# Reordering a head's products in a recurrence and moving a small decay computation two products later in a Fourier stage

## The chip, the cores and the metric

The kernel runs on one core of one Trainium2 chip, in one launch. The metric is the device time in microseconds (us), taken as the median of repeated executions. TensorE is called PE in the rows, VectorE DVE, ScalarE ACT, GpSimd POOL; SyncE (SP) issues the weight loads.

## The reference

Two transformer blocks in float32 on 512 tokens with 16 meta tokens ahead (length L = 528, width 1024). The first block has a forgetting attention (8 heads of 64), a gated linear recurrence (8 heads of 128), and a mixture of 32 experts. The second has a feed-forward layer, a hybrid mixer (a Fourier branch, a short convolution, a two-way gated delta net), and a second feed-forward layer. Two parts matter here.

```python
# the recurrence of the first block, per head of 128; chunks of 64 tokens
f_val = lb + (1.0 - lb) * sigmoid(f_h);  log_f = log(f_val);  k = 1.0 - f_val
q = q_h * 128 ** -0.5;  v = i_h
b = cumsum(log_f, axis=1)                      # within a chunk
o_inter = einsum('bchk,bhkv->bchv', q * exp(b), state)
scores  = sum(q[:, :, None] * k[:, None] * decay, -1)
new_state = exp(b_last)[..., None] * state + einsum('bshk,bshv->bhkv', k_dec, v)
o = rms_norm(o, hgrn_norm_w) * sigmoid(g_h)
# the decays of the second block's delta net, from two small projections
beta = sigmoid(beta_logit);  g = -exp(A_log) * softplus(alpha_logit + dt_bias);  gc = cumsum(g)
```

## The kernel before, in words

**Engines and queues.** Each engine has its own list of instructions, written by a function of its own (`..._pe`, `..._act`, `..._dve`), and runs it in order; semaphores join them. A projection is three float32-rounded products (high by high, high by low, low by high) over eight tiles of 128 rows. So each weight chunk of 128 by 1024, loaded by SyncE into a ring of four places, is first split: ScalarE casts its high half (L556) and VectorE subtracts to get the low half (L562). `ahead_act` and `ahead_dve` do this up to two chunks ahead of the product being made; a load into a place waits until the product that used the place is done.

**The recurrence (about 208 to 580 us, class `Hgrn`).** There are ten stages. In stage h three things run interleaved on every engine: the projections of head h (`project_*`), the levels of head h-1 (`level_*`: the triangular scores, made in one diagonal product and seven level products called level 0 to 6 here), and the output of head h-2 (`output_*`). A stage has eight beats, 0 to 7. In beat n an engine does the level's part, then so many steps of the projection, then the output's part, then some steps more (on ScalarE the output's part comes ahead of both groups of steps). A projection is a generator; each time it is resumed is one call here, numbered from 0. Stages 2, 4 and 6 have four calls a beat, odd stages six: they also hold a gate of the attention branch (`Branch`, calls 34 to 41) and its output product (calls 42 to 45). A head's four products take eight calls each on TensorE: before, f 0 to 7, q 8 to 15, v 16 to 23, g 24 to 31, and at call 32 five transposes (L212) turn v. Products in even stages that are left over after beat 7 follow there.

The accumulators of the projections are two pairs of PSUM banks taken in turn (`pair`); a pair is free once ScalarE has read it: the sigmoid of f (L1170), a scaled copy of q (L1181), a copy of v (L1184), the tanh of g (L1187), the two copies of turned v (L1191, L1192), the tanh of the branch's gate (L937). The level products and the norm's sum of squares take banks 4 and 5 in turn (`row`). In beat 7, after level 6, TensorE takes both banks 4 and 5 for the five transposes of kd (L212), so it waits there for VectorE's masked copy of level 6 (L1343) and for the logarithm (L1227) that reads the norm's sum. The sum is made on TensorE in beat 6; its logarithm and exponential (L1227, L1230) are ScalarE's in beat 7. Per level, VectorE makes differences (L1304, L1305), ScalarE their exponential (L1205), VectorE two products (L1319, L1321) that TensorE's level product reads.

**The Fourier stage (about 1623 to 1748 us, class `ConvFourier`).** Four rounds j, each of four products (x = 3, 0, 1, 2) of about 5.8 us and a small product `small` of the folded rows, in three pairs of banks taken in turn. In round 0 the chunk of the decays' two projections is multiplied too (`row`), VectorE scales the row (L2690), TensorE turns it in six small transposes, and `act1`, `dve1` (L2696 to L2702) make the decays from it; `pe2`, `act2`, `dve2` sum them up in round 1. `busy` issues products whose result nobody reads; 22 of them stand between the row's product and its transposes.

The few lines that order a recurrence stage on ScalarE:

```python
for n in range(8 if h else 0):
    if h < 9: self.level_act(h - 1, n)
    if h >= 2: self.output_act(h - 2, n)
    fill(STEPS[h][0])
    if h < 9 and n == 7: self.turn_act(h - 1)
    fill(STEPS[h][1])
fill(1000)
```

Of the kernel before, what the change touches and what calls it, by code (L numbers as in the profile page):

```python
# [11 lines left out]
ACT = mybir.ActivationFunctionType  # L12
# [3 lines left out]
D, NM, S, L = 1024, 16, 512, 528  # L16
# [951 lines left out]
def load_head(k, W, part, h):  # L968

    for n in "fqvg":  # L970
        x = "qfvg".index(n)
        part[n, h] = W.load(k.a["w_hg"][h, :, 1024 * x:1024 * x + 1024])


class Hgrn:
# [90 lines left out]
    def project_pe(self, h):  # L1066
        k, P = self.k, self.k.P
        yield from self.product_pe("f", h, 0, self.f_sig)
        yield from self.product_pe("q", h, NM, self.q_out)
        yield from self.product_pe("v", h, 0, self.vd_out)  # L1070
        yield from self.product_pe("g", h, NM, self.g_sig)
        self.bank["vturn", h] = b = self.pair()
        P.wait_ge(*self.vd_out.at(h + 1))
        for m in range(4):
            k.tr(k.ps[:, b, 128 * m:128 * m + 128], self.vd[:, NM + 128 * m:NM + 128 * m + 128])
        k.tr(k.ps[0:NM, b + 1, 0:128], self.vd[:, 0:NM]).then_inc(self.vturn.next(), 1)
        k.give((b, b + 1), self.v_out.at(h + 1))
        yield 1

    def level_pe(self, h, beat):  # L1080
# [86 lines left out]
    def project_act(self, h):  # L1167
        k, A, i, i3 = self.k, self.k.A, h % 2, h % 3
        yield from self.product_act("f", h)
        A.activation(two(self.fs), k.wide(self.bank["f", h]), ACT.Sigmoid).then_inc(self.f_sig.next(), 1)  # L1170
        yield 1
        self.W.ahead_act(self.part["q", h])
        yield 1
        yield 1
        k.table(ACT.Ln)
        A.wait_ge(*self.f_val.at(h + 1))
        A.activation(self.lf, self.fs, ACT.Ln).then_inc(self.f_log.next(), 1)
        for _ in range(5):
            yield 1
        A.wait_ge(*self.W.used.at(self.part["q", h] + 1))  # L1180
        A.mul(self.q[:, i, :], k.ps[:, self.bank["q", h], :], 128.0 ** -0.5).then_inc(self.q_out.next(), 1)  # L1181
        yield 1
        yield from self.product_act("v", h)
        A.copy(two(self.vd), k.wide(self.bank["v", h])).then_inc(self.vd_out.next(), 1)  # L1184
        yield 1
        yield from self.product_act("g", h)
        A.activation(self.g[:, i3, :], k.ps[:, self.bank["g", h], :], ACT.Tanh, scale=0.5).then_inc(self.g_sig.next(), 1)  # L1187
        yield 1
        b = self.bank["vturn", h]
        A.wait_ge(*self.vturn.at(h + 1))  # L1190
        A.copy(self.vv[:, i3, 1:5, :].rearrange("p a c -> p (a c)"), k.ps[:, b, :])  # L1191
        A.copy(self.vv[0:NM, i3, 0, :], k.ps[0:NM, b + 1, 0:128]).then_inc(self.v_out.next(), 1)  # L1192
        yield 1

# [21 lines left out]
    def output_act(self, h, n):  # L1216
        k, A, i = self.k, self.k.A, h % 2
        if n == 5:
            A.wait_ge(*self.o_out.at(h + 1))
            A.activation(k.sq[:, 0, 0:S], self.oo[:, i, :], ACT.Square).then_inc(self.o_sq.next(), 1)  # L1220
        if n == 7:
            k.table(ACT.Ln)
# [41 lines left out]
    def project_dve(self, h):  # L1264
# [13 lines left out]
        yield 1  # L1278
        W.ahead_dve(self.part["q", h])
        for _ in range(4):  # L1280
# [3 lines left out]
        for _ in range(4):  # L1284
            yield 1
        for n in "vg":
            W.ahead_dve(self.part[n, h])
            for _ in range(8):
                yield 1
        yield 1  # L1290

# [1344 lines left out]
class Decays:  # L2636
# [18 lines left out]
    def pe1(self, W, i, xh, xl):  # L2655
# [4 lines left out]
        k.give((b, b + 1), self.row_out.at(1))  # L2660
        self.bank["logit"] = b = k.pair()
        k.busy(b + 1, 22)
        P.wait_ge(*self.row_out.at(1))
        for n in range(NC2):
            ins = k.tr(k.ps[0:C2, b, 16 * n:16 * n + 16], self.bl[:, C2 * n:C2 * n + C2])
        ins.then_inc(self.logit.next(), 1)
        k.give((b, b + 1), self.biased.at(1))

# [37 lines left out]
    def pe2(self):  # L2706
        k, P = self.k, self.k.P
        P.wait_ge(*self.g_out.at(1))
        self.bank["cums"] = b = k.pair()
        g = self.g.rearrange("p n c -> p (n c)")  # L2710
        k.mm(k.ps[0:C2, b, 0:48], k.con["ui"][0:C2, 0:C2], g, True, True)
        k.mm(k.ps[0:C2, b, 48:96], k.con["li"][0:C2, 0:C2], g, True, True)
        k.mm(k.ps[0:C2, b, 96:144], k.ones[0:C2, 0:C2], g, True, True).then_inc(self.cums.next(), 1)
        k.give((b, b + 1), self.el_sub.at(1))

# [20 lines left out]
class ConvFourier:  # L2736
# [52 lines left out]
    def pe(self):  # L2789
# [3 lines left out]
        for j in range(4):  # L2793
            for x in (3, 0, 1, 2) if j else (2,):
                w = W.halves_pe(self.part[j, x])
                self.bank[j, x] = b = k.pair()
                linear3(k, b, w, xh, xl, 0, L).then_inc(W.used.next(), 1)
                k.give((b, b + 1), (self.b_out, self.c_out, self.x_raw, self.f_out)[x].at(j + 1))
            if j == 0:
                self.norm.sum_pe()  # L2800
                dec.pe1(W, self.ba, xh, xl)
            if j == 1:
                dec.pe2()
# [29 lines left out]
    def act(self):  # L2833
        k, A = self.k, self.k.A
        W = self.W
        for j in range(4):
# [19 lines left out]
            if j == 0:  # L2856
                W.ahead_act(self.ba)
                self.dec.act1(W, self.ba)
            if j == 1:
                self.dec.act2()  # L2860
# [8 lines left out]
    def dve(self):  # L2869
# [5 lines left out]
        for j in range(4):  # L2875
# [36 lines left out]
            if j == 0:  # L2912
                W.ahead_dve(self.ba)
                self.dec.row_dve(W, self.ba)
                self.dec.dve1()
            if j == 1:
                self.dec.dve2()
# [1151 lines left out]
```

## Time and profile before

| | |
|---|---|
| Median of 3 executions | 2744.97 us (2742.15 to 2747.38) |
| Profiled execution, its own time | 2745.68 us |
| Its span in the trace | 2744.4 us, 38846 instructions |
| TensorE busy | 2655.6 us, 97% of the span |
| VectorE, ScalarE, GpSimd busy | 1295.1, 889.4, 150.1 us |
| Mean granted TensorE clock | 0.994 |

The span runs from the first to the last instruction; 1.3 us of the execution's own time lie around it. An engine's busy time overlaps with that of others. A row of the timeline gives the start, the duration and, in brackets, how long the engine was idle before it and which instruction released it.

### The profile page before, as it was taken

The numbers are of one execution on the slowest core, as the hardware profiler recorded it, in microseconds if no ns is written. First come the engines' busy times: TensorE is split into PE (matmuls) and PEld (weight loads), VectorE is DVE, ScalarE is ACT, GpSimd is POOL, SyncE is SP. The second block draws the span as 40 slices with busy tenths as digits, with TensorE's granted clock in tenths as the row PEclk, the third lists the DMA queues.
The fourth block names the chain that finished last, engine by engine and source line by source line (L and its number), as shares of the span: only waits on it lengthen the run. The fifth ranks groups of instructions, "written<-read, shape, count | busy, mean of one in ns | idle before, by whom it ended". The sixth has DMA issues, their size and how long they took to land.

```text
span 2744.4 us, 38846 instructions
## 1 busy us (share of the span) xinstructions
PE 2655.6 (97%) x16392; PEld 2076.6 (76%) x16392; DVE 1295.1 (47%) x2274; ACT 889.4 (32%) x1319; POOL 150.1 (5%) x201
## 2 busy tenths in 40 slices
PE   8999999999999999999999999999999999999997
PEld 6778888778733333349999999988879776888885
DVE  4445666544423333355344465544544434644444
ACT  4334445333221111133222243444444322431322
POOL 0000000000100000000000000031230400000000
PEclk9999999999999999999999999999999999999998
DMA  3012111134599999963222222211111122222221
GB/s 143 16 63 66 60 59 60 58 139 138 206 414 421 420 420 420 420 273 116 90 88 93 81 80 78 95 58 51 59 59 45 64 93 90 95 93 94 98 87 60
DMA packets 78204, 381.64 MB, mean 139 GB/s; under 512 B 9944, under 2 KB 10200, under 8 KB 52816
## 3 DMA queue, kind: packets, MB, share of 16 engines
q1 hardware_dynamic: 71856, 357.14, 35.1%
q0 software_dynamic: 5456, 20.11, 1.9%
q8 instruction: 132, 2.16, 0.3%
q10 hardware_dynamic: 720, 1.90, 0.2%
q14 instruction: 40, 0.33, 0.0%
HBM read 372.67 MB, written 10.62 MB: 140 GB/s over the span
## 4 chain that ended last, share of the span: by engine, by line
PE 79%; DMA 5%; DVE 4%; ACT 2%; issue 1%; SPq 1%; DVEq 0%; ACTq 0%
PE ps L208 77%; DMA rmore<-in_w_ein 2%; PE ps L212 1%; DMA eahead<-in_w_ein 1%; DMA ring<-in_w_ein 1%; ACT L218 1%; SPq L293 1%; DVE ringr L562 0%; PE ps L1932 0%; ACT ringr L556 0%; DMA ring<-in_w_hg 0%; DVE uT L453 0%; DVE hT L2594 0%; ACT hdd L1205 0%; DVE hT L3875 0%
## 5 line engine op out<-in xcount | busy, mean ns | idle before, releaser
L208 PE MATMUL ps<-uh,ringr 128*128 128x264 f32 (+1 forms) x2256 | 551.8, 339 | 5.8 <-DVE ringr L562 2.6
L208 PEld LDWEIGHTS ps<-uh,ringr 128*128 128x128 f32 x2256 | 364.9, 188 | 49.9 <-issue 5.0
L208 PE MATMUL ps<-buh,ringr 128*128 128x512 f32 (+1 forms) x1312 | 346.6, 350 | 9.2 <-ACT hg L1187 8.1
L208 PE MATMUL ps<-uTr,ringr 128*128 128x512 f32 (+1 forms) x1136 | 349.9, 345 | 0.0
L562 DVE TENSOR_TENSOR ringr<-ring,ringr 128x1024 fp32r<-128x1024 f32 (+1 forms) x217 | 260.5, 1210 | 146.3 <-ACT ringr L556 145.8
L556 ACT CAST ringr<-ring 128x1024 fp32r<-128x1024 f32 (+1 forms) x217 | 221.6, 1036 | 103.7 <-DMA ring<-in_w_fi 45.5
L208 PEld LDWEIGHTS ps<-buh,ringr 128*128 128x128 f32 x1312 | 218.3, 188 | 40.3 <-issue 12.2
L208 PEld LDWEIGHTS ps<-uTr,ringr 128*128 128x128 f32 x1136 | 197.1, 189 | 22.5 <-issue 3.1
L2040 DVE TENSOR_TENSOR hT<-hT,ps 128x512 f32<-128x512 f32 x128 | 87.8, 688 | 182.0 <-PE ps L208 180.9
L208 PE MATMUL ps<-ful,ringr 128*128 128x264 f32 (+1 forms) x648 | 169.4, 322 | 0.0
L208 PE MATMUL ps<-fhh,ringr 128*128 128x264 f32 (+1 forms) x612 | 132.1, 321 | 0.0
L2555 DVE TENSOR_TENSOR fsg<-ps,fsg 128x528 f32<-128x528 f32 (+1 forms) x44 | 30.8, 700 | 196.5 <-PE ps L208 193.1
L208 PEld LDWEIGHTS ps<-ful,ringr 128*128 128x128 f32 x648 | 106.9, 188 | 9.6 <-issue 0.2
L1998 ACT COPY exT<-ps 128x512 f32<-128x512 f32 x32 | 18.8, 587 | 292.8 <-PE ps L1932 292.8
L591 ACT CAST fhh<-fsg 128x528 fp32r<-128x528 f32 (+1 forms) x44 | 27.7, 628 | 234.7 <-DVE fsg L2557 234.7
L208 PEld LDWEIGHTS ps<-fhh,ringr 128*128 128x128 f32 x612 | 95.1, 188 | 9.4 <-issue 0.5
L218 ACT ACT_TABLE_LOAD x78 | 100.1, 1283 | 6.4 <-DMA vec<-in_vec 5.1
L208 PEld LDWEIGHTS ps<-eto,uTr 128*128 128x128 f32 x256 | 38.2, 188 | 77.4 <-issue 71.7
L208 PE MATMUL ps<-eahead,exT 128*64 128x512 f32 x384 | 91.6, 604 | 3.7 <-DMA eahead<-in_w_ein 2.2
L208 PE MATMUL ps<-eto,uTr 128*128 128x512 f32 x256 | 92.4, 444 | 1.6 <-DVE hT L2040 1.4
L208 PE MATMUL ps<-uh,fmore1r 128*128 128x264 f32 x544 | 89.5, 284 | 0.0
L208 PE MATMUL ps<-cuh,ringr 128*128 128x264 f32 x544 | 87.0, 285 | 1.1 <-ACT cuh L484 0.8
(478 smaller groups left out, 4568.6 us busy)
## 6 DMA issues: line engine op xcount, KB each, us to landing
eahead<-in_w_ein SPq DMA_DIRECT2D x48, 1024.0 KB, 22.7
rmore<-in_w_ein SPq DMA_DIRECT2D x44, 1024.0 KB, 23.2
ring<-in_w_ein SPq DMA_DIRECT2D x36, 1024.0 KB, 24.1
ring<-in_w_fi SPq DMA_DIRECT2D x54, 512.0 KB, 3.7
rmore<-in_w_eout SPq DMA_DIRECT2D x26, 1024.0 KB, 26.4
eahead<-in_w_eout SPq DMA_DIRECT2D x22, 1024.0 KB, 26.2
fmore<-in_w_fi SPq DMA_DIRECT2D x34, 512.0 KB, 3.7
ring<-in_w_hg SPq DMA_DIRECT2D x32, 512.0 KB, 3.8
```

What stands on the lines that cost most here:

```text
L208: return self.P.matmul(out, lhsT, rhs, start=start, stop=stop, skip_group_check=True)
L212: return self.P.transpose(out, in_, self.ident[:n, :n])
L218: self.A.preload_act_table_set(SETS[self.set])
L293: self.SP.dma_start(self.slots[s][0][:, 0:n], src).then_inc(self.landed[s], 16)
L556: self.k.A.copy(self.halves(i)[0], self.part(i)).then_inc(self.cast.next(), 1)
L562: self.k.V.tensor_tensor(low, self.part(i), high.bitcast(F32), SUB).then_inc(self.rest.next(), 1)
L591: (self.k.A.copy(h, src) if scale == 1.0 else self.k.A.mul(h, src, scale)).then_inc(self.high.next(), 1)
L1998: A.copy(self.xT[:, e % 2].rearrange("p a c -> p (a c)"), k.ps[:, self.bank("x", e), :]).then_inc(self.x_out.next(), 1)
L2040: k.V.tensor_tensor(h, h, k.ps[:, self.bank("to", n), :], ADD).then_inc(self.added.next(), 1)
L2555: V.tensor_tensor(self.row(s), self.acc(self.bank[i + 1]), self.row(s), MUL).then_inc(self.mixed.next(), 1)
```

## The change

In the recurrence, each head's products are made in the order f, v, q, g where they were made in the order f, q, v, g, and the weight loads follow; the transposes that turn v stand between q and g (call 24 on TensorE, its copies at call 24 on ScalarE) and not behind g; g takes calls 25 to 32. The splitting of g's look-ahead chunk moves from call 24 to call 25. The norm's logarithm and exponential are issued in beat 6, ahead of that beat's calls, and not in beat 7. In the Fourier stage the 22 filler products go; the row's transposes come after the second product of round 1, in bank 6; `act1` and `dve1` move from round 0 to round 1, and `pe2`, `act2`, `dve2` from round 1 to round 2, with bank 7.

```diff
@@ -967,7 +967,7 @@
-    for n in "fqvg":
+    for n in "fvqg":
         x = "qfvg".index(n)
@@ -1066,9 +1066,8 @@
         yield from self.product_pe("f", h, 0, self.f_sig)
+        yield from self.product_pe("v", h, 0, self.vd_out)
         yield from self.product_pe("q", h, NM, self.q_out)
-        yield from self.product_pe("v", h, 0, self.vd_out)
-        yield from self.product_pe("g", h, NM, self.g_sig)
         self.bank["vturn", h] = b = self.pair()
@@ -1076,6 +1075,7 @@
         yield 1
+        yield from self.product_pe("g", h, NM, self.g_sig)
@@ -1169,7 +1169,7 @@
         yield 1
-        self.W.ahead_act(self.part["q", h])
+        self.W.ahead_act(self.part["v", h])
         yield 1
@@ -1177,19 +1177,19 @@
             yield 1
-        A.wait_ge(*self.W.used.at(self.part["q", h] + 1))
-        A.mul(self.q[:, i, :], k.ps[:, self.bank["q", h], :], 128.0 ** -0.5).then_inc(self.q_out.next(), 1)
-        yield 1
-        yield from self.product_act("v", h)
+        A.wait_ge(*self.W.used.at(self.part["v", h] + 1))
         A.copy(two(self.vd), k.wide(self.bank["v", h])).then_inc(self.vd_out.next(), 1)
         yield 1
-        yield from self.product_act("g", h)
-        A.activation(self.g[:, i3, :], k.ps[:, self.bank["g", h], :], ACT.Tanh, scale=0.5).then_inc(self.g_sig.next(), 1)
+        yield from self.product_act("q", h)
+        A.mul(self.q[:, i, :], k.ps[:, self.bank["q", h], :], 128.0 ** -0.5).then_inc(self.q_out.next(), 1)
         yield 1
...
         A.copy(self.vv[0:NM, i3, 0, :], k.ps[0:NM, b + 1, 0:128]).then_inc(self.v_out.next(), 1)
+        yield 1
+        yield from self.product_act("g", h)
+        A.activation(self.g[:, i3, :], k.ps[:, self.bank["g", h], :], ACT.Tanh, scale=0.5).then_inc(self.g_sig.next(), 1)
         yield 1
@@ -1218,7 +1218,7 @@
             A.activation(k.sq[:, 0, 0:S], self.oo[:, i, :], ACT.Square).then_inc(self.o_sq.next(), 1)
-        if n == 7:
+        if n == 6:
             k.table(ACT.Ln)
@@ -1276,18 +1276,19 @@
         yield 1
-        W.ahead_dve(self.part["q", h])
+        W.ahead_dve(self.part["v", h])
         for _ in range(4):
...
             yield 1
-        for n in "vg":
-            W.ahead_dve(self.part[n, h])
-            for _ in range(8):
-                yield 1
-        yield 1
+        W.ahead_dve(self.part["q", h])
+        for _ in range(9):
+            yield 1
+        W.ahead_dve(self.part["g", h])
+        for _ in range(8):
+            yield 1
@@ -2658,13 +2659,16 @@
         k.give((b, b + 1), self.row_out.at(1))
-        self.bank["logit"] = b = k.pair()
-        k.busy(b + 1, 22)
+
+    def logits_pe(self):
+        k, P = self.k, self.k.P
+        self.bank["logit"] = b = 6
+        k.take(6)
         P.wait_ge(*self.row_out.at(1))
...
         ins.then_inc(self.logit.next(), 1)
-        k.give((b, b + 1), self.biased.at(1))
+        k.give((b,), self.biased.at(1))
@@ -2706,12 +2710,13 @@
         P.wait_ge(*self.g_out.at(1))
-        self.bank["cums"] = b = k.pair()
+        self.bank["cums"] = b = 7
+        k.take(7)
         g = self.g.rearrange("p n c -> p (n c)")
...
         k.mm(k.ps[0:C2, b, 96:144], k.ones[0:C2, 0:C2], g, True, True).then_inc(self.cums.next(), 1)
-        k.give((b, b + 1), self.el_sub.at(1))
+        k.give((b,), self.el_sub.at(1))
@@ -2796,10 +2801,12 @@
                 k.give((b, b + 1), (self.b_out, self.c_out, self.x_raw, self.f_out)[x].at(j + 1))
+                if j == 1 and x == 0:
+                    dec.logits_pe()
             if j == 0:
...
                 dec.pe1(W, self.ba, xh, xl)
-            if j == 1:
+            if j == 2:
                 dec.pe2()
@@ -2855,8 +2862,9 @@
                 W.ahead_act(self.ba)
+            if j == 1:
                 self.dec.act1(W, self.ba)
-            if j == 1:
+            if j == 2:
                 self.dec.act2()
@@ -2912,8 +2920,9 @@
                 self.dec.row_dve(W, self.ba)
+            if j == 1:
                 self.dec.dve1()
-            if j == 1:
+            if j == 2:
                 self.dec.dve2()
...
                 self.turned_dve(j)

```

## Rows read from the trace of the kernel before

**Rows 1.** The page's chain that ended last, by engine, whole span
```profile
PE 79%; DMA 5%; DVE 4%; ACT 2%; issue 1%; SPq 1%; DVEq 0%; ACTq 0%
```

**Rows 2.** Who TensorE waited for, 190 to 640 us: total, times, longest
```profile
PE ps L208 <- ACT hg L1187: 8.1, 4, 2.3
PE ps L212 <- ACT rb L1227: 5.5, 3, 1.9
```

**Rows 3.** Timeline, TensorE, stages 1 and 3: start, us, instruction, [idle before]
```profile
249.90 1.00 PE L208 MATMUL ps<-hQl,hKl 128*128 128x64 f32 x8
...
327.07 0.47 PE L208 MATMUL ps<-buh,ringr 128*128 128x512 f32 x1 [2.26 <-ACT hg L1187]
...
334.46 1.00 PE L208 MATMUL ps<-hQl,hKl 128*128 128x64 f32 x8
```

**Rows 4.** Timeline, ScalarE in stages 1 and 3, VectorE in stage 3
```profile
245.05 1.05 ACT L556 CAST ringr<-ring 128x1024 fp32r<-128x1024 f32 x1 [1.22 <-DMA ring<-in_w_hg]
...
328.10 1.05 ACT L556 CAST ringr<-ring 128x1024 fp32r<-128x1024 f32 x1 [0.55 <-DMA ring<-in_w_hg]
...
332.12 0.42 DVE L1321 TENSOR_TENSOR hQl<-hdd,hq 128x256 f32<-128x256 f32 x1
```

**Rows 5.** Timeline, TensorE, beats 6 and 7 of stage 4
```profile
370.32 1.02 PE L208 MATMUL ps<-sq,o 128*128 128x512 f32 x2
...
372.57 1.00 PE L208 MATMUL ps<-hQl,hKl 128*128 128x64 f32 x8
...
374.38 0.76 PE L212 MATMUL ps<-con,hkd 128*128 128x128 f32 x5 [0.82 <-DVE hsc L1343]
```

**Rows 6.** Timeline, ScalarE and VectorE, same beats and the stage's end
```profile
370.92 1.25 DVE L562 TENSOR_TENSOR ringr<-ring,ringr 128x1024 fp32r<-128x1024 f32 x1
371.38 0.69 ACT L1227 ACTIVATE rb<-ps,eps 128x512 f32<-128x512 f32 x1 [0.76 <-PE ps L208]
...
373.61 0.72 DVE L1343 COPY_PREDICATED hsc<-con,ps 128x64 f32<-128x64 int32 x4 [1.44 <-PE ps L208]
...
378.53 0.59 ACT L1191 COPY hv<-ps 128x512 f32<-128x512 f32 x1
...
379.01 0.25 ACT L1192 COPY hv<-ps 16x128 f32<-16x128 f32 x1
```

**Rows 7.** Timeline, TensorE, Fourier stage
```profile
1653.50 5.07 PE L208 MATMUL ps<-o 128*128 128x128 f32 x44
...
1659.77 1.54 PE L208 MATMUL ps<-dfs,cue 128*88 128x128 f32 x12
1661.07 0.49 PE L208 MATMUL ps<-cuh,ringr 128*128 128x264 f32 x2
...
1697.70 0.64 PE L208 MATMUL ps<-cuh,ringr 128*128 128x264 f32 x4
```

**Rows 8.** Timeline, VectorE, Fourier stage
```profile
1656.39 2.35 DVE L562 TENSOR_TENSOR ringr<-ring,ringr 128x1024 fp32r<-128x1024 f32 x2
...
1660.11 0.20 DVE L2696 TENSOR_TENSOR ntm<-ps,vec 88x48 f32<-88x48 f32 x1 [0.76 <-ACT nbe L2676]
...
1662.82 0.68 DVE L2941 COPY ccs<-ps 88x512 f32<-88x512 f32 x1
...
1689.70 0.17 DVE L2720 COPY ngc<-ps 88x24 f32<-88x24 f32 x1
...
1690.77 0.68 DVE L2941 COPY ccs<-ps 88x512 f32<-88x512 f32 x1
...
1695.40 1.23 DVE L562 TENSOR_TENSOR ringr<-ring,ringr 128x1024 fp32r<-128x1024 f32 x1 [1.03 <-ACT ringr L556]
```

**Rows 9.** Busy time by stretch; after POOL: granted TensorE clock, DMA share, GB/s
```profile
292.00:337.00 45.00, 41.20 (x270) 36.72 (x268) 25.73 (x75) 21.84 (x31) 0.00 (x0) 1.00 0.19 60
565.00:568.00 3.00, 0.32 (x1) 0.00 (x0) 1.33 (x3) 1.70 (x3) 0.00 (x0) 1.00 0.48 167
568.00:572.00 4.00, 3.69 (x18) 3.69 (x19) 1.48 (x2) 2.33 (x2) 0.00 (x0) 0.57 0.00 2
```

## The prediction

> **What bounds the kernel now.** The chain that ended last is read first: 79% of it is TensorE and only a few per cent lie with any other engine [rows 1]. So the time is TensorE's work plus its waits, and since the change takes no product out but the 22 fillers, I look for TensorE's waits, who ends each, and what is queued behind. The list of waits over the recurrence has two entries that the change aims at: 8.1 us in four waits for the tanh of g (L1187), all in odd stages, and 5.5 us in three for the norm's logarithm in beat 7 (L1227), in stages 3, 5 and 7 [rows 2]. In the Fourier stage the reader is to see the fillers followed by the small product and round 1 [rows 7]. Then the timelines of VectorE and ScalarE say what comes last once a wait is gone.
>
> **Odd stages.** The bank pairs alternate, so the branch's gate takes the pair of g just after g is done, while ScalarE still has a table load before its tanh: 2.26 us idle in stage 3 [rows 3]. In the new order turned v holds that pair, and its copies run seven calls earlier; the tanh's pair is next taken at call 42. This wait goes. What is late next: the weight chunk two ahead of the gate is loaded into g's place, so its load starts when g ends, and ScalarE stands at the cast until it lands (328.10, stage 3). Behind the cast in both queues are VectorE's low half, the differences of level 6, their exponential and the two products; the last starts at 332.12 [rows 4]. TensorE started level 6 at 334.46, and without the 2.26 us it would be there at 332.20 [rows 3]. A wait of this kind releases TensorE about 0.57 us after the start of L1321. And g now ends later: the five transposes, 0.76 us in the row and some 0.55 until the next product can follow [rows 5], come ahead of it. They shorten beat 4 by 0.15, since they stand for a step of 0.70, but beat 5 holds three steps of g and not two; g's end moves by about +0.7 - 0.15 - 0.08 = +0.47. So level 6 starts at 332.12 + 0.47 + 0.57 = 333.16: 1.30 us won, 0.96 given back. In stage 1 the same chain from the cast at 245.05 takes 332.12 + 0.57 - 328.10 = 4.59 us, and level 6 is due at 245.05 + 0.47 + 4.59 = 250.1, where it started at 249.90 [rows 3, 4]: nothing won, 0.2 lost. In stage 7 no such load exists (the next chunks are the branch's and the place is further off), so its whole wait goes, a little under the mean of the four, 8.1 / 4 [rows 2]: 1.95.
>
> The logarithm in beat 6 ends before level 6 does, even with the added table load (the branch's tanh now follows it; odd stages load five tables and not four, in ScalarE's idle time). Then the transposes in beat 7 wait only for the masked copy, which costs 0.82 us in stage 4 where nothing else is late [rows 5], and not 5.5 / 3 = 1.83 [rows 2]: 1.0 us in each of stages 3, 5 and 7. Sum: stage 1 +0.2; stages 3 and 5 -2.3 each; stage 7 -2.95; together -7.35.
>
> **Even stages.** Here the root costs something. In beat 6 ScalarE now does, in this order: the exponential of level 6, the wait for the norm's sum, logarithm, exponential, the two copies of turned v, and only then the cast of the look-ahead chunk (call 25). Before, the cast went first, so that VectorE's low half ran at 370.92, in time for the masked copy at 373.61 [rows 6]. VectorE's call 25 also lies in beat 6, so it stands at that cast, and the masked copy of level 6 and with it TensorE's transposes stand behind. In stage 4: the sum, at 370.32 [rows 5], comes 0.2 earlier (transposes 0.55 in place of a step). The logarithm so starts at 371.18 and not 371.38, the exponential at 371.91, the copies at 372.45 and 372.93 (0.48 apart as at 378.53 and 379.01), the cast at 373.09, the low half, behind the cast's 1.05 [rows 4], at 374.18, the masked copy at 375.33 [rows 6]. The transposes follow it by 374.38 - 373.61 = 0.77, at 376.1, where they stood at 374.38: +1.7 us [rows 5, 6]. The wait grows from 0.82 to 2.7 us. Three such stages: +5.1. Bounds: nothing, if ScalarE were not held there, and 2.0 each if nothing runs closer than in those rows.
>
> **Stage 0, 8, 9.** In stage 0 g's bank waits for q's copy, which only the 0.55 us of transposes cover: +0.15. In stages 8 and 9 no projection is left and the logarithm's new place has nothing queued behind it that TensorE needs: 0. The recurrence comes to -7.35 + 5.1 + 0.15 = -2.1.
>
> **Fourier stage.** The fillers start at 1653.50; small product and round 1 start at 1659.77 and 1661.07 [rows 7]. Now the small product follows at 1653.50 and takes 1.3 us, to 1654.8. Its bank pair is then the one of round 0's c, long read. The first product of round 1 needs its low half, which VectorE makes only at 1656.39, behind round 0's convolution [rows 8]; such a release comes about 1.28 us after the start, at 1657.67. So -3.4 us, with 2.9 us idle where the fillers stood. The six transposes return later, +0.37; `pe2` costs the same in round 2 as in round 1. Next: `dve1` in round 1 takes 1662.82 - 1660.11 = 2.7 us with its waits for ScalarE, where `dve2` took 1690.77 - 1689.70 = 1.1 [rows 8]. With the 0.37 this delays all of VectorE's and ScalarE's round 2 by 2.0; the low half for the third product of round 2, at 1695.40, moves to 1697.4 and would release TensorE at 1698.7 [rows 8], but TensorE arrives at 1697.9 (in the row at 1697.70 the second half is that product) less 0.07: a new wait of 0.9 us [rows 7]. Round 3 has 1.4 us in hand. Sum: -3.4 + 0.4 + 0.9 = -2.1.
>
> **The clock.** Four waits are now long: 2.7 us in stages 2, 4 and 6 and 2.9 in the Fourier stage. After 3.0 us without products near 565 us the granted clock of the next 4 us was 0.57, that is mostly at the lower of its levels, 1.2 GHz; stage 3, with waits of 2.26 and 1.85 us, kept 1.00, 2.4 GHz [rows 9]. A fall costs 4.0 x (1 - 0.57) = 1.7 us if TensorE is the bound behind it, as it is in all four places. How many come is not in the rows: bounds 0 and 4; the new waits lie nearer to 3.0 than to 2.26 but below it, and I take two: +3.4.
>
> The Trainium skill speaks against removing the fillers: "TensorE: Matmul & The Clock Gate", section "Why this matters for your kernels", asks that there be no long idle gaps between bursts of products, since the clock then drops back. The fall near 565 us agrees with it; the page does not settle gaps of 2.7 us, and by its advice alone the sum would lie between those for no fall and for four.
>
> **The sum.** -2.1 - 2.1 + 3.4 = -0.8 us. The profiled execution, 2745.7 us, would come to 2744.9; it lies 0.7 above the median of the runs, so the median is forecast at 2744.2. What can be told from no change here is about 0.2%, 5.5 us.
>
> **The rivals.**
> *No fall of the clock.* For it: waits up to 2.26 us caused none. Against: the new waits are longer, and those in the even stages stand behind a small product. Time: 2744.97 - 4.2 = 2740.8. Chance 0.18.
> *The even stages don't wait.* If ScalarE and VectorE get the cast done in the shadow of level 6, 5.1 us and three chances of a fall vanish: -2.1 - 5.1 - 2.1 = -9.4, 2735.6. Against it stands the order of the two queues; for it only that I may have misplaced call 25. Chance 0.13.
> *Slower: the low clock repeats.* The place is the even stages: with products at half speed after each long wait, the clock could fall twice in each of the three, and once in the Fourier stage. Seven falls cost 11.9: -4.2 + 11.9 = +7.7, 2752.7. It decides from six falls on (+6.0). For it: each of these waits is followed by small products and a second, short wait. Against: behind the fall near 565 the products ran on and no second one came. Chance 0.08.
> *The odd stages don't gain.* The tanh wait would turn wholly into the wait for the load, as I expect in stage 1; then -4.6 for stages 3, 5 and 7 stays out, and the time is 2748.8. The rows at 332.12 and 334.46 speak against it. Chance 0.08.
>
> **Chances and range.** One to four falls with the rest as summed: 0.53, from 2742.5 to 2747.6. Faster by over 0.2% (below 2739.5): the second rival, and some 0.06 of the first with smaller waits than worked out: 0.19. Slower by over 0.2% (above 2750.5): the repeated falls and 0.03 of the fourth: 0.11. Within: 0.70. The range leaves out most of the second rival and the third: 2736.5 to 2749.5.
>
> **What would show it.** In the changed kernel's waits: no wait for L1187 but at most 0.2 us; none for L1227; in stages 3 and 5 about 1 us for L1321 at level 6; in stages 2, 4 and 6 some 2.7 us for L1343 ahead of the transposes of kd, with ScalarE's cast starting after L1192 in beat 6; in the Fourier stage 2.9 us for L562 after the first small product and 0.9 us in round 2; the granted clock below 1 just after some of these. Wrong would make it: a masked copy of level 6 that isn't held up, a release other than L562 in round 1, or falls of another number or price.

## The result, and the profile after

The changed kernel takes 2757.22 us (median of 6 runs, 2755.29 to 2759.05), the kernel before beside it 2747.06 (6 runs, 2742.15 to 2749.06). The ratio is 1.0038, 95% interval 1.0028 to 1.0048: slower by 0.38%, about 10 us, where 2744.2 was forecast (from 2744.97, the median of the first three runs of the kernel before). The profiled execution took 2757.95 us with a span of 2756.6, 12.2 more than the span before.

First the page of the changed kernel: the head, TensorE's busy row and the chain that ended last, which answers to [rows 1].

```profile
span 2756.6 us, 38761 instructions
...
PE 2662.4 (97%) x16348; PEld 2079.4 (75%) x16348; DVE 1294.7 (47%) x2274; ACT 891.1 (32%) x1321; POOL 149.6 (5%) x201
...
PE 78%; DMA 5%; DVE 5%; ACT 2%; issue 1%; SPq 0%; DVEq 0%; ACTq 0%
```

The bound is still TensorE. Next, who it waited for in the recurrence (190 to 660 us; total, times, longest), which answers to [rows 2].

```profile
PE ps L212 <- DVE hsc L1344: 9.7, 5, 2.7
PE ps L208 <- DVE hsc L1344: 3.5, 2, 1.8
PE ps L208 <- DVE hQl L1322: 3.1, 4, 1.9
...
PE ps L212 <- issue: 2.6, 3, 0.9
```

Both entries of [rows 2] are gone, as they should be. In their place stands the masked copy (L1344; L1343 before), ahead of the transposes of kd (L212) and, twice, ahead of level 6 (L208). TensorE's timeline in stages 3 and 4, which answers to [rows 3, 5]:

```profile
334.12 1.02 PE L208 MATMUL ps<-sq,o 128*128 128x512 f32 x2
...
339.06 1.10 PE L208 MATMUL ps<-hQl,hKl 128*128 128x64 f32 x8 [1.84 <-DVE hsc L1344]
341.03 0.86 PE L212 MATMUL ps<-con,hkd 128*128 128x128 f32 x5 [0.86 <-issue]
...
377.79 1.00 PE L208 MATMUL ps<-hQl,hKl 128*128 128x64 f32 x8
381.46 0.76 PE L212 MATMUL ps<-con,hkd 128*128 128x128 f32 x5 [2.67 <-DVE hsc L1344]
```

The two engines behind it: ScalarE in beats 6 and 7 of stage 4, which answers to [rows 6],

```profile
376.59 0.69 ACT L1227 ACTIVATE rb<-ps,eps 128x512 f32<-128x512 f32 x1 [1.50 <-PE ps L208]
...
377.85 0.57 ACT L1188 COPY hv<-ps 128x512 f32<-128x512 f32 x1
378.32 0.25 ACT L1189 COPY hv<-ps 16x128 f32<-16x128 f32 x1
378.47 1.04 ACT L556 CAST ringr<-ring 128x1024 fp32r<-128x1024 f32 x1
```

and VectorE, the end of level 6 in stage 3 and then beats 6 and 7 of stage 4.

```profile
337.96 0.42 DVE L1322 TENSOR_TENSOR hQl<-hdd,hq 128x256 f32<-128x256 f32 x1
338.29 0.72 DVE L1344 COPY_PREDICATED hsc<-con,ps 128x64 f32<-128x64 int32 x4
...
379.55 1.23 DVE L562 TENSOR_TENSOR ringr<-ring,ringr 128x1024 fp32r<-128x1024 f32 x1 [3.02 <-ACT ringr L556]
380.69 0.72 DVE L1344 COPY_PREDICATED hsc<-con,ps 128x64 f32<-128x64 int32 x4
```

In stage 4 the reader sees the forecast queue: root's logarithm, two copies of turned v, cast, low half, masked copy, transposes. From the logarithm to the transposes it takes 381.46 - 376.59 = 4.87 us, where 376.1 - 371.18 = 4.92 was worked out. In stage 3 level 6 is not released by the products on VectorE (337.96) but by the masked copy of level 5 queued behind them (338.29).

TensorE in the Fourier stage, which answers to [rows 7], and at the end of the last mixer, where its output products start:

```profile
1662.23 1.47 PE L208 MATMUL ps<-dfs,cue 128*88 128x128 f32 x12
1666.39 0.81 PE L208 MATMUL ps<-cuh,ringr 128*128 128x264 f32 x2 [2.69 <-DVE ringr L562]
...
1705.49 0.51 PE L208 MATMUL ps<-cuh,ringr 128*128 128x264 f32 x2 [0.65 <-DVE ringr L562]
...
2299.97 2.17 PE L208 MATMUL ps<-o 128*128 128x128 f32 x18
2307.22 0.76 PE L208 MATMUL ps<-uh,ringr 128*128 128x512 f32 x1 [5.08 <-DVE mgb L3881]
```

The last row has no word in the prediction. In the kernel before, the same place of the timeline reads:

```profile
2291.69 2.17 PE L208 MATMUL ps<-o 128*128 128x128 f32 x18
2295.26 0.47 PE L208 MATMUL ps<-uh,ringr 128*128 128x512 f32 x1 [1.40 <-DVE mgb L3872]
...
2300.24 0.50 PE L208 MATMUL ps<-uh,ringr 128*128 128x512 f32 x1 [0.96 <-DVE uTr L597]
```

At last the granted clock, by stretches of the changed kernel chosen right behind the long waits (length, PE busy, then clock, DMA share, GB/s). They answer to [rows 9].

```profile
250.00:260.00 10.00, 9.14 (x41) 0.83 0.19 60
292.00:302.00 10.00, 9.68 (x51) 0.83 0.16 52
341.00:351.00 10.00, 9.97 (x47) 0.83 0.18 54
381.00:391.00 10.00, 9.54 (x50) 0.83 0.18 55
430.00:440.00 10.00, 10.00 (x47) 0.83 0.17 54
470.00:480.00 10.00, 9.60 (x51) 0.83 0.18 54
1666.00:1676.00 10.00, 9.61 (x68) 0.84 0.10 27
2302.00:2312.00 10.00, 4.92 (x15) 0.66 0.19 54
```

The matching eight stretches of the kernel before (from 250, 289, 337, 374, 422, 460, 1661 and 2295 us) all show 1.00. A stretch of 10 us at 0.83 has lost 1.7 us of full clock; that is called one fall below, and 0.66 over 10 us a double one. The products of 128x512 show it one by one, 0.63 in place of 0.39 us: 1.2 for 2.4 GHz. It is not one execution's doing: the mean clock was 0.988 to 0.990 in all six runs of the changed kernel, and 0.991 to 0.995 in 24 runs of the kernel before (those beside turn_back, below).

Where the 12.2 us come from can be read from the start of the transposes of kd, before and after:

| stage | before | after | behind by | added in the stage | of it the fall just before | the rest | forecast |
|---|---|---|---|---|---|---|---|
| 1 (with 0) | 251.76 | 251.87 | 0.11 | +0.11 | 0 | +0.1 | +0.35 |
| 2 | 288.84 | 292.32 | 3.48 | +3.37 | 1.7 | +1.7 | +1.7 |
| 3 | 337.31 | 341.03 | 3.72 | +0.24 | 1.7 | -1.5 | -2.3 |
| 4 | 374.38 | 381.46 | 7.08 | +3.36 | 1.7 | +1.7 | +1.7 |
| 5 | 422.78 | 429.98 | 7.20 | +0.12 | 1.7 | -1.6 | -2.3 |
| 6 | 459.89 | 470.40 | 10.51 | +3.31 | 1.7 | +1.6 | +1.7 |
| 7 | 508.06 | 517.01 | 8.95 | -1.56 | 1.7 | -3.3 | -2.95 |

The recurrence is 8.95 us longer: -1.3 by its waits and +10.2 by six falls, if each costs the full 1.7. The Fourier stage gives 0.6 us back (8.72 behind at its start, 8.10 at its end), with one fall in it. From its first product with a chunk (cuh) to its last it takes 111.2 us before and 110.6 here, but 109.3 in fou_only and keep_clock (below), which have no fall there: so -1.9 by its waits and some +1.3 by the fall. At the last mixer's start the kernel is 8.0 us behind, behind its output products 12.2 (2357.17 against 2344.98).

### The profile page after: what moved, and what is told of

It reads as the page before. It is cut to its first block, busy times and chain, and to the rows that moved or that the text cites. A ratio compares the mean times of both kernels' runs of the same rounds, so it can differ in the third digit from the quotient of the medians.

```text
span 2756.6 us, 38761 instructions
## 1 busy us (share of the span) xinstructions
PE 2662.4 (97%) x16348; PEld 2079.4 (75%) x16348; DVE 1294.7 (47%) x2274; ACT 891.1 (32%) x1321; POOL 149.6 (5%) x201
## 4 chain that ended last, share of the span: by engine, by line
PE 78%; DMA 5%; DVE 5%; ACT 2%; issue 1%; SPq 0%; DVEq 0%; ACTq 0%
PE ps L208 75%; DMA eahead<-in_w_ein 3%; PE ps L212 1%; DMA rmore<-in_w_ein 1%; DMA ring<-in_w_ein 1%; DVE ringr L562 1%; PE ps L1933 0%; ACT ringr L556 0%; DVE hsc L1344 0%; ACT hdd L1205 0%; DMA ring<-in_w_hg 0%; ACT L218 0%; SPq L293 0%; DVE hT L2595 0%; DVE uT L453 0%
## 5 line engine op out<-in xcount | busy, mean ns | idle before, releaser
L208 PE MATMUL ps<-uh,ringr 128*128 128x264 f32 (+1 forms) x2256 | 552.3, 340 | 8.5 <-DVE mgb L3881 5.1
L208 PEld LDWEIGHTS ps<-uh,ringr 128*128 128x128 f32 x2256 | 365.8, 189 | 52.0 <-issue 8.7
L208 PE MATMUL ps<-uTr,ringr 128*128 128x512 f32 (+1 forms) x1136 | 352.8, 347 | 0.0
L208 PE MATMUL ps<-buh,ringr 128*128 128x512 f32 (+1 forms) x1312 | 349.2, 353 | 1.4 <-PE ps L208 0.7
L208 PEld LDWEIGHTS ps<-buh,ringr 128*128 128x128 f32 x1312 | 220.3, 190 | 32.6 <-issue 3.6
L208 PEld LDWEIGHTS ps<-uTr,ringr 128*128 128x128 f32 x1136 | 198.5, 190 | 23.6 <-issue 3.1
L208 PE MATMUL ps<-ful,ringr 128*128 128x264 f32 (+1 forms) x648 | 169.4, 322 | 0.0
L208 PE MATMUL ps<-fhh,ringr 128*128 128x264 f32 (+1 forms) x612 | 132.1, 321 | 0.0
L208 PEld LDWEIGHTS ps<-ful,ringr 128*128 128x128 f32 x648 | 106.9, 188 | 9.6 <-issue 0.2
L208 PEld LDWEIGHTS ps<-fhh,ringr 128*128 128x128 f32 x612 | 95.1, 188 | 9.4 <-issue 0.5
L208 PEld LDWEIGHTS ps<-eto,uTr 128*128 128x128 f32 x256 | 38.3, 188 | 77.4 <-issue 71.7
L208 PE MATMUL ps<-eahead,exT 128*64 128x512 f32 x384 | 91.7, 604 | 3.4 <-DMA eahead<-in_w_ein 1.9
L208 PE MATMUL ps<-eto,uTr 128*128 128x512 f32 x256 | 92.5, 444 | 1.6 <-DVE hT L2041 1.4
L208 PE MATMUL ps<-cuh,ringr 128*128 128x264 f32 x544 | 88.5, 288 | 4.5 <-DVE ringr L562 3.3
L208 PE MATMUL ps<-uh,fmore1r 128*128 128x264 f32 x544 | 89.4, 284 | 0.0
```

Of the source, the lines that this page charges most:

```text
L208: return self.P.matmul(out, lhsT, rhs, start=start, stop=stop, skip_group_check=True)
```

## The experiments

All are compared with the kernel before on the same chip. The runs were made on several chips, so two kernels measured on different ones are compared by their ratios to the kernel before. In the edits h is the head: the levels belong to stage h + 1, the output to stage h + 2. A filler is a product of `busy`; a row of the timeline counts each as two instructions (x20 for 10). "behind the long waits" means the places of the table and windows above.

**The two halves and the banks at the mixer's end.** The Fourier stage of the changed kernel draws two bank pairs fewer from a counter that only `first_pe` sets back. The last mixer's output products go on with it, so their first pair is another one. `MixerEnd` fills its banks in the order 4, 5, 6, 7, 0, 1, 2, 3, with the bank of the network's last sum put at the end, and VectorE's gated products (L3881) leave them in that order: the first pair is free after the sixth of them in the kernel before, after the eighth and last in the changed one.

```
         k.busy(banks[0], 9)
+        k.turn += 2          # turn_back: in the changed kernel
+        k.turn += 1          # turn_on_before: in the kernel before
         for m in range(8):
```

> The changed kernel with the counter that hands out bank pairs moved on by two ahead of the last mixer's output products, so that they take the same pairs as in the kernel before; nothing else differs. Theory: the Fourier stage of the changed kernel draws two pairs fewer, and the output products therefore begin in other banks, which the gated products leave last; the wait of 5.08 us at 2307.22 goes back to the two of 1.40 and 0.96 us, the low clock of 6.8 us behind it goes too, and the run is 4.0 us shorter than the changed kernel: 0.9986 of it, about 2753.2. Rival: the wait comes from something that arrives late (a chunk, a turned value), whichever banks are used; then no difference, 2757.2.

Measured: 2755.64 us (7 runs), 1.0026 (1.0014 to 1.0037). That is 0.0012 under the changed kernel's 1.0038, 3.3 us, where 4.0 was expected; the two intervals overlap, so the time alone doesn't settle it. But its timeline has the two waits of before again:

```profile
2306.41 0.47 PE L208 MATMUL ps<-uh,ringr 128*128 128x512 f32 x1 [1.39 <-DVE mgb L3882]
2311.39 0.51 PE L208 MATMUL ps<-uh,ringr 128*128 128x512 f32 x1 [0.97 <-DVE uTr L597]
```

> The kernel before with nothing changed but the same counter moved on by one ahead of the last mixer's output products: they begin in the pair that they have in the changed kernel. Theory of the banks: +4.0 us, about 2751.0, ratio 1.0015, with one wait of some 5.1 us for the gated products and a low clock behind it. Rival (something else of the change is late there): no difference.

Measured: 2750.74 us (11 runs), 1.0014 (1.0005 to 1.0023), 3.8 us: as expected, with nothing else edited. TensorE's timeline and its clock by stretches:

```profile
2305.28 0.77 PE L208 MATMUL ps<-uh,ringr 128*128 128x512 f32 x1 [5.08 <-DVE mgb L3873]
```

```profile
243.00:253.00 10.00, 8.66 (x38) 0.83 0.15 52
329.00:339.00 10.00, 9.46 (x39) 0.83 0.06 23
2301.00:2311.00 10.00, 5.72 (x15) 0.66 0.17 48
```

The same 5.08 us and the same 0.66: the rival is out. The first two stretches tell more. They lie in stages 1 and 3 of the recurrence as it was before, behind the waits for the tanh of g, and the clock fell there; in the trace of the kernel before it didn't.

> The kernel before with the edits of the recurrence alone. Theory: all of the +8.9 us by which the trace of the changed kernel is behind when it enters the Fourier stage comes from them: six falls of the clock and waits of 2.67 us in stages 2, 4 and 6; 2755.9, ratio 1.0032. My forecast for this part, without falls, was -2.1 us. Rival: the falls depend on more than the order in this stage and come in another number; each one fewer takes 1.6 to 1.7 us off.

```
 kernel before, with only the edits of load_head, project_pe, project_act,
 project_dve and output_act
```

Measured: 2756.12 us (6 runs), 1.0032 (1.0020 to 1.0044). The theory's ratio. Its output products have the waits of 1.40 and 0.96 us again. The clock lost as much as in the changed kernel, but not in the same places: double falls in stages 1 and 3 (0.66 from 252 and from 341 us), single ones in stages 5 and 6 (0.83 from 430 and from 470), none in 2 and 4.

> The kernel before with the edits of the Fourier stage alone, the counter of bank pairs put right ahead of the last mixer's output products. Theory: as in the trace of the changed kernel, -0.6 us, waits of 2.69 and 0.65 us, one fall of the clock: 2746.4, ratio 0.9998. Rival: without the delays of the recurrence no fall comes there, then -2.3 us: 2744.7, ratio 0.9992.

```
 kernel before, with only the edits of logits_pe, pe2 and the Fourier stage's
 pe, act and dve, and k.turn += 2 at the mixer's end
```

Measured: 2745.47 us (11 runs), 0.9997 (0.9988 to 1.0006). It has the waits of 2.70 and 0.67 us. Its profiled execution shows no fall behind them (1.00 over 1660 to 1670 us) and one in stage 3 (0.83 over 326 to 336 us), which it doesn't touch. The stage itself is 1.9 us shorter than before. Whether a fall is typical there this run leaves open; between -0.6 and -2.3 us its interval doesn't choose.

**Is it the clock, or the waits?** Fillers inside the waits leave every wait's end where it is and take only the idleness.

```
+        if beat == 7 and h in (0, 2, 4):     # ahead of level 6
+            k.busy(6, 7)
...
         if beat == 7:
+            if h < 6:                        # ahead of the transposes of kd
+                k.busy(6, 10 if h % 2 else 3)
             k.take(4, 5)
...
+            if j == 0:                       # Fourier stage, behind the small product
+                k.busy(6, 10)
```

> The changed kernel with the bank pairs of the last mixer put right (turn_back), and with fillers (products of 128x128 on ones, result unread) in bank 6 inside the long waits: 10 ahead of the transposes of kd in stages 2, 4 and 6, 7 ahead of level 6 and 3 ahead of the transposes in stages 1, 3 and 5, and 10 in the Fourier stage between the small product of round 0 and the first product of round 1. By the fillers of the kernel before (22 in 5.07 us) they last 2.3, 1.6, 0.7 and 2.3 us, less than the waits they lie in. Every wait stays; only TensorE's idleness in them goes. Theory: the clock's falls are what the long waits cost beyond themselves; seven falls of 1.7 us go, 11.9 us, from turn_back's 2755.6 (or 2753.2 by its trace's own account): between 2741.3 and 2743.7, ratio 0.997 to 0.9985. Rival: the waits themselves, not the clock, hold the time; then within 1 us of turn_back, ratio 1.0026.

Measured: 2742.36 us (11 runs), 0.9981 (0.9972 to 0.9990), 0.0045 or 12.4 us under turn_back; 11.9 was expected. Stage 4 in its timeline, and its clock:

```profile
374.10 2.45 PE L208 MATMUL ps<-o 128*128 128x128 f32 x20
376.93 0.77 PE L212 MATMUL ps<-con,hkd 128*128 128x128 f32 x5 [0.38 <-DVE hsc L1348]
```

```profile
250.00:260.00 10.00, 9.38 (x55) 6.87 (x54) 5.00 (x18) 3.04 (x6) 0.00 (x0) 1.00 0.31 99
376.00:386.00 10.00, 9.62 (x65) 8.47 (x65) 6.43 (x19) 4.60 (x7) 0.00 (x0) 1.00 0.17 53
1657.00:1667.00 10.00, 9.54 (x79) 9.50 (x79) 8.25 (x12) 3.77 (x5) 0.00 (x0) 1.00 0.18 54
```

The masked copy still releases the transposes 0.38 us behind the last filler, so the wait is there in full, and the clock stays at 2.4 GHz: 1.00 over 200 to 560 us and over 1640 to 1740. The mean clock of the 11 runs is 0.993 to 0.995, where turn_back's seven have 0.989 to 0.990. The falls, not the waits, made the recurrence slower: with the clock kept and the banks right the kernel is 0.19% faster than before. By the trace, though, its recurrence ends about where it did: the transposes of stage 7 start at 507.68, 0.4 us ahead of before and 9.3 ahead of the changed kernel. So six falls cost between 9.3 and the 10.2 us of the table, and the new order wins 0.4 to 1.3 us there, less than the 2.1 forecast. The Trainium skill, "TensorE: Matmul & The Clock Gate", section "Why this matters for your kernels", asks to avoid long idle gaps between bursts of products. By that advice, the runs agree; what they add is that waits of 2.67 us, and pairs of 1.6 to 2.2 and 0.86 us, were already long enough here in many cases, though not in all: turn_back has its waits of 2.67 us in stages 2, 4 and 6 too, and the clock behind them is 1.00.

**Where the root belongs.**

```
         (on turn_back, output_act)
-        if n == 6:
+        if n == 7:                           # root_seven
+        if n == (6 if h % 2 else 7):         # root_odd: beat 6 in odd stages alone
```

> turn_back with the norm's root back in beat 7 in every stage; the new order of the head's products stays. Theory: the wait of 2.67 us in stages 2, 4 and 6 falls back to 0.82, and their falls of the clock go (3 x 3.36 us less); the transposes of kd in stages 3 and 5, and in 7, wait for the root again, 1.0 us more in each. Against turn_back: -10.1 + 3.0 = -7.1 us, 2748.5 to 2746.1. Rival: another part of the new order holds the masked copy in the even stages; then its wait stays and the run gets no shorter.

Measured: 2744.94 us (11 runs), 0.9989 (0.9980 to 0.9998), 0.0037 or 10.2 us under turn_back. That is more than the 7.1 expected, but the two intervals leave some 4 us either way. The trace is 7.4 us ahead of turn_back's at the transposes of stage 7 (509.88 against 517.30); the rest comes behind the recurrence, in part because turn_back's trace has a fall in the Fourier stage and this one none. TensorE's waits in the recurrence:

```profile
PE ps L212 <- DVE hsc L1344: 4.1, 5, 0.9
PE ps L208 <- DVE hsc L1344: 3.4, 2, 1.7
PE ps L208 <- DVE hQl L1322: 3.2, 4, 2.0
...
PE ps L212 <- ACT rb L1227: 1.9, 1, 1.9
```

The waits of 2.7 us are 0.9 at most, so the root in beat 6 did hold the masked copy in the even stages. And in beat 7 the root is waited for once, not three times: in stages 3 and 5 level 6 is late by 1.7 us anyway, and the logarithm runs beside that. Two of the three gains of 1.0 us for which I had priced the root's move were not there to be had. The falls are not as expected: two double ones, in stages 1 and 5 (0.66 from 252 and from 423 us), and none in stage 3. That is four of turn_back's six, and not three.

> turn_back with the root at beat 6 in odd stages and at beat 7 in even stages. Theory: even stages as in root_seven, odd stages as in the changed kernel, so -10.1 us against turn_back and 3.0 under root_seven: 2743.1 to 2745.5, ratio 0.9985 to 0.9993. Three falls, behind the waits for level 6 in stages 1, 3 and 5, remain. Rival: the root in beat 6 wins nothing in odd stages, since level 6 is late there either way; then equal to root_seven.

Measured: 2743.65 us (11 runs), 0.9989 (0.9980 to 0.9998). 1.3 us below root_seven by the medians, inside their intervals; the expected difference of 3.0 is too large for the reason just given, that of 1.0 for stage 7 fits. Falls are left here too, and again four in sum where three were expected: a double one in stage 1 (0.66 from 250 to 260 us), single ones in stages 3 and 5; one more stands in the Fourier stage.

> root_odd with the fillers of keep_clock in stages 1, 3 and 5 and in the Fourier stage. Theory: four falls fewer than root_odd, 6.8 us: 2736.3 to 2738.7, ratio 0.996 to 0.9969, faster than both kernels. Rival: fillers delay products that could have started (bank 6 or the queue), then no better than root_odd.

```
 root_odd, with keep_clock's lines for h in (0, 2, 4) and for the Fourier stage
```

Measured: 2737.28 us (6 runs), 0.9967 (0.9955 to 0.9979), 6.4 us under root_odd where 6.8 was expected. Clear of both kernels. The clock is 1.00 over 200 to 556 us and over 1640 to 1740.

**What the falls cost the kernel before.**

```
 kernel before
+        if m < 4:                            # Branch.pe, ahead of the gate's pair
+            k.busy(6, 8)
...
+            if h in (2, 4, 6):               # level_pe, beat 7, ahead of k.take(4, 5)
+                k.busy(6, 5)
```

> The kernel before with fillers in its own waits of stages 1, 3, 5 and 7: 8 (1.8 us) ahead of the branch's gate, where it waits for the tanh of g, and 5 (1.15 us) ahead of the transposes of kd, where stages 3, 5 and 7 wait for the root's logarithm. No wait ends earlier. Three traces of this recurrence (before, turn_on_before, fou_only) show no, two and one fall of the clock there, so its waits of 1.8 to 2.4 us bring a fall in some executions. Theory: without that idleness no fall is left, on average one fall, 1.7 us: 2746.2, ratio 0.9994. Rival: the falls there had another cause; then ratio 1.000 and falls as before in stages 1 and 3.

Measured: 2746.90 us (12 runs, 2742.45 to 2748.36), 0.9995 (0.9986 to 1.0004), with the kernel before at 2742.44 to 2753.21 in 17 runs. The effect expected, 0.0006, is within the interval and so is none: inconclusive on the time. Its trace has no fall in stages 1 to 7, but neither had that of the kernel before, so it proves nothing. Its slowest runs are 5 us nearer to its fastest, in 12 runs against 17.

**The two waits left, level 6 and round 1.**

```
-            self.bank["sum", h] = b = self.row()
+            self.bank["sum", h] = b = 7      # sum_seven, on combo; 4 fillers, not 7
+            k.take(7)                        # ahead of level 6 in stages 3 and 5
```

> combo with the norm's sum in bank 7 and not in the two banks of the level products, so that level 6 takes the other bank than level 5; 4 fillers and not 7 ahead of level 6 in stages 3 and 5. Theory: level 6 in stages 3 and 5 no longer waits for the masked copy of level 5 (1.84 us), only for the products on VectorE (L1322), as my forecast assumed: about 1.2 us, so 0.6 less twice, -1.2 us against combo's 2737.3: 2736.1. Rival: both end together, or the copy of level 6 behind it takes the gain back; then as combo.

Measured: 2736.45 us (6 runs), 0.9960 (0.9945 to 0.9974). By the time alone not to be told from combo. The trace shows it: combo's fillers ahead of level 6 in stage 3 start at 332.12 and its transposes at 335.89, 3.77 us; here

```profile
332.19 1.05 PE L208 MATMUL ps<-o 128*128 128x128 f32 x8
333.45 1.08 PE L208 MATMUL ps<-hQl,hKl 128*128 128x64 f32 x8 [0.21 <-DVE hQl L1327]
334.36 0.89 PE L208 MATMUL ps<-o 128*128 128x128 f32 x6
335.40 0.74 PE L212 MATMUL ps<-con,hkd 128*128 128x128 f32 x5
```

3.21 us, 0.56 less, and the releaser of level 6 is the product on VectorE: my forecast's chain holds once level 6 has a bank of its own.

```
         (on combo, Fourier stage, dve)
+            if j == 0:
+                W.ahead_dve(self.ba)         # ahead of conv_dve, no longer behind sc_out
             conv_dve(V, self.sc[:, j, :], self.xb[:, i], w, self.conv, self.x_out.last())
...
-            if j == 0:                       # Fourier stage, pe: no fillers
-                k.busy(6, 10)
```

> combo without the Fourier fillers, and with VectorE's low halves for the decays' product and the first product of round 1 ahead of round 0's convolution and not behind it. Theory: the wait of 2.7 us at the first product of round 1 goes (the low half is there 5 us earlier), no fall there: 2737.3 - 2.7 + 0 = 2734.6, or one less if round 2's wait grows by what is won. Rival: the low half then waits for ScalarE's cast instead, and VectorE's convolution with it; then no gain, 2737 or more.

Measured: 2736.05 us (6 runs), 0.9958 (0.9942 to 0.9974), where 2734.6 was expected; by the time alone not to be told from combo's 0.9967 either. The trace shows the gain: the Fourier stage takes 106.3 us from its first product with a chunk to its last, where combo takes 109.3. VectorE's two low halves start right behind L2914, ahead of the convolution, and round 1 no longer waits:

```profile
1649.03 0.71 DVE L2914 TENSOR_TENSOR cxb<-cxb,crb 128x528 f32<-128x528 f32 x1
1649.66 2.35 DVE L562 TENSOR_TENSOR ringr<-ring,ringr 128x1024 fp32r<-128x1024 f32 x2
1651.93 0.49 DVE L2634 TENSOR_SCALAR msc<-cxb,vec 128x528 f32<-128x528 f32 x1
```

> sum_seven and low_early together. Theory: 1.2 and 2.7 us under combo: 2733.4, ratio 0.995 to 0.9955 of before. Rival: as for each of them.

Measured: 2733.40 us (6 runs, 2732.71 to 2734.94), 0.9951 (0.9936 to 0.9966): 13.5 us, 0.49%, under the kernel before, and by the ratios 4.4 us under combo, where 3.9 was expected; the intervals of the two overlap, so the step from combo rests on the traces.

## Why the prediction was wrong, step by step

**What bounds the kernel: right.** TensorE does, and the changes came about as its waits and their follow-ups.

**Odd stages: half right.** The tanh waits and those for the logarithm went. Stage 1 came out at 249.94 for level 6, where 250.1 was worked out, stage 7 at -3.3 for -2.95. The step that failed is "level 6 starts at 332.12 + 0.47 + 0.57 = 333.16: 1.30 us won, 0.96 given back". I took L1321 as the releaser. But levels and sum share two banks, the sum of beat 6 lies between level 5 and level 6, and so level 6 takes level 5's bank and waits for its masked copy, 0.6 us further on. Stages 3 and 5 gained 1.5 and 1.6 us and not 2.3. sum_seven shows 0.56 us of this in stage 3; the remaining 0.2 us or so I have not traced.

**Even stages: right.** +1.7 each was forecast, 1.6 to 1.7 came; the wait is 2.67 for 2.7 us, in the queue order forecast. root_seven shows the cause of the wait.

**Fourier stage: right.** Waits of 2.69 and 0.65 us for 2.9 and 0.9, the stage -1.9 us without a fall, in fou_only and keep_clock, for -2.1.

**The clock: wrong, and the larger part of the error.** The step was "How many come is not in the rows: bounds 0 and 4 ... I take two: +3.4". Seven came, 11.5 us (six of 1.7 and one of 1.3): 8.1 more. The count was wrong, and hardly the price, which the windows give as 1.7 again, though in the Fourier stage only 1.3 reached the time. I counted only waits near 3 us. In the odd stages 1.89, 1.84 and 1.64 us ahead of level 6 and 0.86 behind its small products come to 2.5 to 2.75 us as well, and behind each of these three pairs the clock fell. That the two waits count as one is my reading; no run took away one of a pair. I took stage 3 of the kernel before, with 2.26 and 1.85 us and a clock of 1.00 [rows 9], as proof that such waits are harmless. It was one execution: two other traces of the same recurrence have falls there (turn_on_before in stages 1 and 3, fou_only in stage 3). keep_clock shows that the falls are the cost. The slower rival had the right number, "Seven falls cost 11.9", and its 2752.7 comes nearest, but by luck, for it had the wrong place: I let it decide through second falls in the even stages and gave it 0.08. In this trace each of stages 1 to 6 has one.

**What was not in the sum at all: the bank pairs.** +4 us at the end of the last mixer. I priced the bank pairs that the decays give back only in the Fourier stage itself ("Its bank pair is then the one of round 0's c"), and didn't follow the counter to its next reader. turn_on_before shows the whole effect by itself. Of the 5.08 - 1.40 = 3.7 us more of waiting 0.96 comes back at the next product, and the low clock behind it adds 5.0 x (1 - 0.60) = 2.0, by the granted clock over 2307 to 2312 us; the rest of the 3.4 us lies inside the wait. That makes 4.7, where 4.2 was measured; the last 0.5 I have not traced.

Together: -1.3 - 1.9 + 11.5 + 4.2 = +12.5, where the spans differ by 12.2 and -0.8 was forecast.

What stays open: why the same waits bring a fall in one execution and not in the next. In turn_back the six falls of the recurrence came as three double ones in stages 1, 3 and 5 (0.66 over 251 to 261 us), with 1.00 behind the waits of stages 2, 4 and 6 (294 to 304, 383 to 393 and 472 to 482 us), in rec_only as two double and two single ones, in the changed kernel as six; the sum was the same. In these three traces a stage of even number has a fall exactly where the odd stage ahead of it had a single one. So how much of the lost clock belongs to which wait can't be read from its place: without the waits of 2.67 us (root_seven, root_odd) two of six went, with every one of the waits filled or gone (keep_clock, combo) all six. A run with fillers in the even stages alone would tell more and was not made. Nor is it settled how often one comes behind round 1 of the Fourier stage: it did in the changed kernel, in turn_back (0.84 over 1669 to 1679 us) and in root_odd, and didn't in fou_only and root_seven.

## What to carry to other kernels

Price a new wait twice, once for its length and once for the clock behind it, and count two waits with a few small products between them as a candidate too; fillers shorter than the wait kept the clock here, and one trace in which the clock holds is no proof that it does. When an edit draws fewer or more buffers from a running counter, follow the counter to its next user, in the next stage or far on. Before moving an operation to the front of a queue, look at what stands behind it in the same beat: here one root ahead of one cast held a copy on another engine, and was worth moving in one stage of seven only.

## What the runs showed of the hardware

Waits of 1.9 to 2.3 us brought the lower clock in some executions of one and the same instruction stream and not in others: in stages 1 and 3 of the recurrence as before, none, two and one in three traces. Falls go with this kernel's spread, 2742 to 2753 us: of its 17 runs beside before_filled the fastest, 2742.44 us, has a mean clock of 0.995 and the slowest, 2753.21, one of 0.990 (rounded to thousandths); 0.005 of 2745 us is some 14 us, enough for the whole spread. A wait of 2.67 us brought one in the changed kernel each time, in stages 2, 4 and 6, and in turn_back none behind the same three. Fillers of 128x128 that nobody reads, 10 in 2.4 us, kept 2.4 GHz through such waits (keep_clock).
